# A mixture-of-experts weight stream with 16 raw and 4 high buffers, blocks in TensorE's order of use

## What is computed

```python
def swiglu(t, w_up, w_down):
    gate, up = split_cols(t @ w_up, (w_down.shape[0], w_down.shape[0]))
    return (jax.nn.silu(gate) * up) @ w_down

y = swiglu(u_pad[tok], w_exp_up[e], w_exp_down[e])      # up: 1024 x 512, down: 256 x 1024
acc = acc.at[tok].add(y.astype(jnp.float32) * w_of_slot[slots][:, None])
```

## Time and profile before

| | us |
|---|---|
| runs | 1229.41, 1229.84, 1231.94 |
| median | 1229.84 |
| the profiled execution | 1231.59 |
| its span | 1229.3 |
| TensorE busy (matmuls) | 1137.4 |
| VectorE busy | 900.8 |
| ScalarE busy | 723.1 |
| GpSimd busy | 222.1 |

### The profile page before, as it was taken

How to read it: one execution, slowest core, us unless ns; L and a number is a source line. 1 busy time by engine, 2 the same in 40 slices (tenths; PEclk the granted TensorE clock), 3 DMA queues, 4 the chain that set the end, 5 groups by cost and what they waited for, 6 DMA issues and landing times.

```text
span 1229.3 us, 16284 instructions
## 1 busy us (share of the span) xinstructions
PE 1137.4 (93%) x5707; PEld 860.9 (70%) x5707; DVE 900.8 (73%) x1133; ACT 723.1 (59%) x926; POOL 222.1 (18%) x145
## 2 busy tenths in 40 slices
PE   4999998989999899998999999999999999999893
PEld 3699997766777688774666666666666667666662
DVE  4585468544433576578899999998989899999881
ACT  7543343333333422413788888888878788888781
POOL 1000000000000000001232333333433233333421
PEclk9999999999999999999999999999999999999997
DMA  6413232221212234267899999999999999999982
GB/s 214 134 53 103 86 95 69 69 69 34 68 35 68 81 120 137 86 257 272 298 355 362 366 364 369 367 362 369 375 370 368 370 366 378 373 377 362 370 291 33
DMA packets 74495, 285.58 MB, mean 232 GB/s; under 512 B 10868, under 2 KB 33416, under 8 KB 49620
## 3 DMA queue, kind: packets, MB, share of 16 engines
q1 hardware_dynamic: 59716, 251.16, 54.2%
q0 software_dynamic: 14736, 33.87, 11.6%
HBM read 272.39 MB, written 29.38 MB: 245 GB/s over the span
## 4 chain that ended last, share of the span: by engine, by line
PE 58%; DMA 14%; DVE 12%; ACT 7%; issue 7%; SPq 0%; DVEq 0%; POOL 0%; ACTq 0%; POOLq 0%
PE bank L1452 47%; DMA arena<-in_w_exp_up_dram 12%; DVE low L1356 4%; ACT high L554 4%; DVE gatheredT L1363 2%; PE bank L1620 2%; DMA out_dram<-arena 2%; ACT arena L554 2%; PE bank L1647 2%; PE bank L1833 1%; PE bank L1531 1%; PE bank L1778 1%; PE bank L1632 1%; DVE arena L1370 1%; DMA arena<-in_x_dram 1%
## 5 line engine op out<-in xcount | busy, mean ns | idle before, releaser
L1356 DVE TENSOR_TENSOR low<-arena,high 128x2048 fp32r<-128x2048 f32 x192 | 435.3, 2287 | 51.7 <-ACT high L554 51.5
L554 ACT ACTIVATE high<-arena 128x2048 fp32r<-128x2048 f32 x192 | 363.9, 1918 | 23.0 <-DMA arena<-in_w_exp_up_dram 22.2
L1452 PE MATMUL bank<-high,gatheredT 128*96 128x512 f32 x1024 | 327.0, 401 | 19.2 <-DVE gatheredT L1363 17.9
L516 POOL DMA_INDIRECT arena<-u_rows,arena x64 | 103.3, 1614 | 742.1 <-DVE arena L1351 563.5
L1452 PEld LDWEIGHTS bank<-high,gatheredT 128*96 128x96 f32 x1024 | 161.5, 163 | 93.2 <-issue 23.9
L1452 PE MATMUL bank<-low,gatheredT 128*96 128x512 f32 x512 | 203.2, 397 | 0.0
L1452 PE MATMUL bank<-high,hidT 128*96 128x512 f32 x512 | 163.6, 401 | 1.5 <-ACT arena L554 1.5
L524 POOL DMA_INDIRECT out_dram<-arena x64 | 112.7, 1761 | 250.1 <-DMA out_dram<-arena 148.5
L1452 PE MATMUL bank<-hT_high,front_split 128*128 128x512 f32 x448 | 146.4, 409 | 0.8 <-DVE hT_low L892 0.8
L554 ACT ACTIVATE arena<-bank 96x512 f32<-96x512 f32 (+4 forms) x217 | 107.7, 533 | 62.9 <-PE bank L1452 28.3
L1452 PEld LDWEIGHTS bank<-low,gatheredT 128*96 128x96 f32 x512 | 83.4, 163 | 36.5
(11 more groups left out here) (253 smaller groups left out, 1402.5 us busy)
## 6 DMA issues: line engine op xcount, KB each, us to landing
arena<-in_w_exp_up_dram SPq DMA_DIRECT2D x128, 1024.0 KB, 22.7
arena<-in_w_exp_down_dram SPq DMA_DIRECT2D x64, 1024.0 KB, 18.8
arena<-in_w_in_dram SPq DMA_DIRECT2D x14, 1024.0 KB, 5.4
arena<-in_w_in_dram SPq DMA_DIRECT2D x10, 768.0 KB, 4.4
arena<-in_w_branches_dram SPq DMA_DIRECT2D x4, 1024.0 KB, 5.0
arena<-in_w_out_dram SPq DMA_DIRECT2D x4, 1024.0 KB, 5.0
arena<-in_x_dram SPq DMA_DIRECT2D x4, 512.0 KB, 5.5
arena<-in_w_mem_kv_dram SPq DMA_DIRECT2D x2, 1024.0 KB, 5.0
```

The lines of the kernel that those rows point to most:

```text
L516: pool.indirect_dma_start(gathered[0:ROWS, e % 2, :], None, u_dram, bass.IndirectOffsetOnAxis(ap=index[0:ROWS, e:e + 1], axis=0), bounds_c ...
L554: return nc.scalar.activation(o, i, ACT.Copy, **kw)
L1356: v.tensor_tensor(low_part[q % SLOTS], raw[q % SLOTS], high_part[q % HIGHS].bitcast(F32), ALU.subtract).then_inc(low_done, 1)
L1452: ins = mm(bank, left[a], right[b], start=first and q == 0, stop=last and q == 2)
```

## The change

- `SLOTS` 12 to 16 and `HIGHS` 6 to 4: two high buffers and the places of routing data (`gates_at` + 4096 and + 6144, `ib_at`, `ib_at` + 2048) become raw buffers. `place`, `w_high`, `w_low` and the token numbers move to other corners, since loads now land where they were.
- Blocks are numbered by position in TensorE's order of use: up 0, up 1, down 0, up 2, down 1, ... (`up_at`, `down_at`). Loads, conversions and products all take buffers by this position.
- A load at position k waits for `block_used` to reach k - 15, that is for the block that had its buffer. In the first round positions 10 and 11 wait for `set_done`, 12 and 13 for `folded`, 14 and 15 each for two of the output stores, which now have two semaphores.
- Stores of output rows: two after the load at position 10, then a wait until the first gather has landed (`gather_in[0]`), then loads 11 to 13, then the other two stores.
- A conversion waits for `block_used` of the block four positions before it.
- `TURN` 4 to 16: 16 experts written out at the start, a loop of two turns (SyncE: three), 16 at the end. The old `TURN` that sized the routing tables becomes `DEAL` = 4.

Cut to its core:

```diff
-TURN = 4
+DEAL = 4
+TURN = 16
 BLOCKS = 3
-SLOTS, HIGHS = 12, 6
-LEAD = 5
+SLOTS, HIGHS = 16, 4
+ROUNDS = BLOCKS * TURN // SLOTS
...
+def up_at(n, j, first=False):
+    return j if first and n == 0 else BLOCKS * n - 1 + j
+
+def down_at(n, last=False):
+    return BLOCKS * n + (2 if last and n == TURN - 1 else 4)
...
-            def load_expert_block(e, n, j, u0):
-                s = (BLOCKS * n + j) % SLOTS
-                if not isinstance(e, int):
-                    sp.wait_ge(block_used, u0 + (BLOCKS + 2 - SLOTS if j == 2 else j - SLOTS + (n == 0)))
...
+            def load(src, k, u):
+                s = k % SLOTS
+                if not isinstance(u, int) or k >= SLOTS:
+                    sp.wait_ge(block_used, u + (k - SLOTS + 1))
+                elif s < 4:
+                    sp.wait_ge(x1_done, 2 * NT)
+                elif s < 6:
+                    sp.wait_ge(front_low, S0 + s - 3)
+                elif s < 10:
+                    sp.wait_ge(s_up, NT)
+                elif s < 12:
+                    sp.wait_ge(set_done, 1)
+                elif s < 14:
+                    sp.wait_ge(folded, 1)
                 else:
-                    sp.wait_ge(out_stored, 16 * NT)
+                    sp.wait_ge(out_stored[s - 14], 16 * NT // 2)
+                sp.dma_start(raw[s].rearrange("p k n -> p (k n)"), src).then_inc(raw_in[s], 16)
+
+            def store_rows(k, u):
+                if isinstance(u, int) and k in (10, 13):
+                    for t in (0, 1) if k == 10 else (2, 3):
+                        sp.wait_ge(out_ready, t + 1)
+                        sp.dma_start(out[0, t * P:(t + 1) * P, :], x_tok[:, t, :]).then_inc(out_stored[t // 2], 16)
+                    if k == 10:
+                        sp.wait_ge(gather_in[0], 16)
+
+            def load_turn(e, n, u, first=False):
+                for j in range(2):
+                    load(up_src[:, e, j, :], up_at(n, j, first), u)
+                    store_rows(up_at(n, j, first), u)
+                if not first or n:
+                    load(dn_src[:, e - 1, :], down_at(n - 1), u)
+                    store_rows(down_at(n - 1), u)
...
+            def high(k, u, round0):
+                if isinstance(u, int) and u + k < HIGHS:
+                    act.wait_ge(s_up, NT)
+                else:
+                    act.wait_ge(block_used, u + (k - HIGHS + 1))
+                act.wait_ge(raw_in[k % SLOTS], round0 * 16 + 16 * (k // SLOTS + 1))
+                copy(high_part[k % HIGHS], raw[k % SLOTS]).then_inc(high_done, 1)
...
             def expert(n, m, u, round0, start=False, last=False):
...
-                for j in range(min(blocks, 2)):
-                    high(q + j, u + (LEAD + j), round0)
+                if ups:
+                    high(up_at(n + 2, 0), u, round0)
+                    high(up_at(n + 2, 1), u, round0)
...
-                if blocks > 2:
-                    high(q + 2, u + (LEAD + 2), round0)
+                if downs:
+                    high(down_at(n + 1, last), u, round0)
```

More of the change, by code:

```diff
@@ L180, in build @@
         s_hid = at(qa_at, NT, FH)
-        ro = [at(ib_at + n * 256, NT, E) for n in range(16)]
-        (score, choice, masked, masked2, picked, weight, place) = ro[0:7]
+        (score, choice, masked, masked2, picked, weight) = [at(ib_at + n * 256, NT, E) for n in range(6)]
+        place = at(square_at + P, NT, E)
         router_bias = at(ib_at + 11 * 256, E)
@@ new lines, in load_turn, with load_pass @@
+            def load_turn(e, n, u, first=False):
[5 more added lines that the diff above has]
+                    store_rows(down_at(n - 1), u)
+            def load_pass(u0):
+                for n in range(TURN):
+                    load_turn(n, n, u0, True)
+                with sp.Fori(1, E // TURN) as g:
+                    for n in range(TURN):
+                        load_turn(g * TURN + n, n, u0 + g * (BLOCKS * TURN))
+                load(dn_src[:, E - 1, :], BLOCKS * TURN - 1, u0 + BLOCKS * (E - TURN))
@@ L474, in _ @@
                     with sp.If(fullest > r * ROWS):
[L475 to L479 removed]
+                        sp.wait_ge(index_ready, r + 1)
+                        load_pass(r * (BLOCKS * E))
         @block.gpsimd
@@ L535, in expert_pass @@
                     if isinstance(r, int) and e == 0:
-                        pool.wait_ge(out_stored, 16 * NT)
+                        for h in range(2):
+                            pool.wait_ge(out_stored[h], 16 * NT // 2)
                     scatter(e, r)
@@ L823, in expert @@
             def expert(n, m, u, round0, start=False, last=False):
-                q, blocks = BLOCKS * n + LEAD, ahead(n, last)
+                ups, downs = not last or n + 2 < TURN, not last or n + 1 < TURN
                 act.wait_ge(hidT_done, m + 1)
```

170 lines of the change are left out of this document (72 added, 98 removed).

## The result

The changed kernel takes 1243.61 us (median of 4 runs, 1242.35 to 1247.3), the kernel before beside it 1229.62 (4 runs, 1228.5 to 1231.94). The ratio is 1.0117, 95% interval 1.0092 to 1.0141: slower by 14 us, where 9 us faster was forecast. The profiled execution has a span of 1241.7 us.

A forecast was written before the change was run, and what follows sets the result against it. DMA and TensorE were both full, with DMA taken to set the end. A 3.25 MB head start at 367 GB/s gives 8.9 us, other costs zero or hidden: 1229.84 - 8.9 = 1220.9 us, range 1216.9 to 1229.0.

The forecast's parts named there:

- The bytes: Loads before 603.8 us: earlier issue and fuller DMA give a head start of 3.25 MB.
- ScalarE's waits for loads: Sign of being right: conversions' waits for loads fall from 22 us to under 8, all late.
- From bytes to time: End of the DMA-limited experts: 3.25 MB at 367 GB/s moves it 8.9 us earlier.
- The bound for the high ring: Conversions with 4 high buffers: closed loop of 9.5 us against 9.605, costing 0 to 0.05 us per expert.
- the third rival: Head start lost again through longer gather or scatter waits or SyncE idling: 1229 to 1231, no change; chance 0.11.
- Turns of 16: Loops of 16 experts: same instructions, fewer jumps; 1 us taken, hidden by later DMA waits.
- the second rival: Long loop body stalls an engine on an instruction fetch at expert 32: about 1225; chance 0.14, shared with tighter high buffers.
- Order of use: Conversions permuted into TensorE's order: more slack, no gain by itself, cost zero.
- The hold: SyncE holds loads 11 to 15 and last stores until the first gather lands, in 4.0 to 4.8 us: cost zero.
- the cushion of late loads: Some 3 us of remaining DMA waits in the last experts, hiding up to 3 us of PE, ScalarE or VectorE costs.

The follow-up runs named there:

- a_rot: Changed kernel with loops rotated by two experts, so experts 2 to 49 are real loop code on TensorE, VectorE and ScalarE: median 1239.5 us (1223.73 to 1245.11).
- b_t16_two: Kernel before with turns of 16 and a second DRAM sum for odd experts' scatters, final sum of the two left out: 1230.0 us.
- a_two: Changed kernel with odd experts' scatters into a second DRAM sum, so two can be in flight, final sum left out: 1225.5 us.
- b_turn16: Kernel before with turns of 16 experts instead of 4, nothing else changed: 1247.3 us, ratio 1.0134.
- a_t4: Changed kernel with turns of 4 instead of 16 and hence 12 raw buffers: 1226.5 us, ratio 0.9979.
- a_t4_nohold: Changed kernel with turns of 4 and 12 raw buffers, loads and stores no longer waiting for the first gather: 1232.4 us.
- a_slow2: Changed kernel with two redundant TensorE transposes more in every expert: 1251.2 us (1242.14 to 1251.85).
- a_dynpe: Changed kernel with TensorE's experts 2 to 15 in a loop of one pass, which was built without register steps: 1246.6 us.
- a_lowsplit: Changed kernel with each of VectorE's long subtractions cut into two halves: 1241.3 us (1235.5 to 1248.53).
- a_slow1: Changed kernel with one redundant TensorE transpose more in every expert: median 1236.2 us (1225.67 to 1247.53).
- b_t16_rot: Kernel before with turns of 16 and its loops rotated by two experts: 1246.8 us (1243.03 to 1255.71).
- b_peelpe: Kernel before with TensorE's first 16 experts as straight code instead of the first 4: median 1234.1 us (1226.38 to 1241.51).
- a_t4_lowsplit: Changed kernel with turns of 4, 12 raw buffers and VectorE's subtractions cut in two: 1227.4 us.

## Why the prediction was wrong

**What held.** The bytes: 564 to 603.8 us ran at 340 GB/s instead of 242, which is 3.9 MB in 39.8 us, against 3.25 forecast. Some of it is chance. In this execution VectorE took over the routing products at 563.64, 2.9 us earlier than before, though the work up to there is the same; over the profiles of all kernels this instant lies between 562.4 and 568.9.

```profile
563.64 1.49 DVE L1358 TENSOR_TENSOR own_part<-bank,arena 128x432 fp32r<-128x432 f32 x3 [0.36 <-PE bank L1831]
```

Counted from there, over 37.2 us each, it is 334 GB/s against 238, or 3.6 MB. DMA share 1.02 and 381 GB/s up to 603.8; ScalarE's waits for loads are gone; conversions wait 1.7 us at the longest for the ring of 4, 7.6 us in all; the loop jumps stay at 76 to 211 ns.

**From bytes to time** the forecast was too high even without the chain. The short execution of a_rot, with all parts of the change, has a span of 1221.9 against 1229.3, 7.4 us less; counted from the routing products on (564.43 and 566.57) it is 5.2. With the chain cut, the change without its turns is worth 1230.0 - 1225.5 = 4.5 us (b_t16_two and a_two). Forecast were 8.9, so about half of this term came. Where the rest went no run shows; in a_two loads are late again, 16.0 us in 14 waits. The bound for the high ring was added up a little low as well: with halves of 1.86 and 2.28 us the loop makes 9.55, not 9.5.

**The step that failed** is the third rival's, in two places. "Scatters already land in 8.9 us, longest 10.5, near the period of 9.6, and they run one after the other": the period of a scatter is not its landing but its landing and the 0.8 us until the next one starts, and with that it was 9.67 in the first stretch of before (600 to 690 us, below): 0.7 us of slack per expert became next to none. I had compared a duration with a period.

```profile
L524 POOL DMA_INDIRECT out_dram<-arena x10: 1442/1442/1792, 600.3 to 687.3; - x10
...
DMA to landing us min/median/max: 8.1/8.7/9.6
```

(687.3 - 600.3) / 9 = 9.67. The chain could do slightly better than that: over the next 13 experts, up to 820.8 us, it kept to (820.8 - 696.6) / 13 = 9.55:

```profile
L524 POOL DMA_INDIRECT out_dram<-arena x14: 1442/1442/1751, 696.6 to 820.8; - x14
```

In the second place I wrote of scatters of 9.7 us that "the pace would be theirs: 1229 to 1231, no change", and against it "the DMA share is 1.02 in both versions, so their competition is the same". The landing does not hang on the DMA share alone. At the same share of 1.02 it was 8.7 us where scatters lag by 6 us (a_rot) and 9.4 where they lag by 10 (the changed kernel), with issues of 1.47 and 1.90. Without the issues that is 7.2 and 7.5, so the larger part of the difference is how long VectorE holds up GpSimd, a cost that the DMA share doesn't show. So the chain, once it sets the pace, is slower than the pace that it takes over, and the result is a loss. What was missing was a rival that says so: from expert 16 on 47 x (10.19 - 9.6) = 28 us behind a pace of 9.6, where late loads cost the kernel before 12.3.

**Turns of 16** were the term of the sum that was mis-sized: 1 us forecast, 17 measured in the kernel before (b_turn16), and some 2 without the chain (b_t16_two). I looked for the cost in jumps and code fetches, the second rival. There was none: what the turns did first was a gain, 0.09 us per expert, and it goes with the fewer register steps (a_rot, in loop code, is back at 9.62). TensorE can't use it, as the scatters don't follow.

**Order of use and the high ring**: order, ring and hold together, with 12 buffers, are worth 3.3 us (a_t4), in the direction forecast and not to be told further apart. **The hold** was put at no cost, since the gather "lands in 4.0 to 4.8 us when DMA is light". That held: in a_t4 it lands in 4.1, and without the hold the kernel is 5.9 us slower (a_t4_nohold), of which the later first tokens are 2.9.

**The range** ended at 1229 because every cost that I let stand was bounded by the cushion of late loads. But the cushion of the scatters, the third resource near its limit, was not worked out at all.

**When the lag jumps.** In the profiles of kernels with one chain the lag of the scatters stays below 2 us (before, for 49 experts), rests at 6 to 8, or at 9 to 11, and at 9 to 11 the result copies wait. The expert at which it first passes 9 goes with the time of that execution:

| profiled execution | lag first over 9 at expert | us |
|---|---|---|
| a_slow2 | 11 | 1250.7 |
| a_dynpe | 13 | 1250.0 |
| the changed kernel | 14 | 1243.5 |
| a_lowsplit | 26 | 1235.5 |
| a_slow1 | 50 | 1225.7 |
| a_rot | never | 1223.7 |
| a_t4 | never | 1225.4 |

So the wide spreads within a series need no third cause: it is enough that the jump comes sooner or later. One profile a kernel can't prove that.

**What stays open.** Shown: the changed kernel's time is set by the chain of scatters (a_two, b_t16_two), a scatter comes every 9.7 or every 10.2 us in the profiles, and turns of 16 bring on the second in most executions. Only argued: why. Pace alone doesn't decide (a_slow2, b_t16_rot), nor does straight code alone (b_peelpe, a_rot). Whether the issues that VectorE lengthens decide, a_lowsplit can't tell, since its halves often held them up like one subtraction. That the second began at expert 9, inside a subtraction, is one observation in one profile. The best complete version is a_t4, the change with turns of 4 (a_t4_lowsplit is the same within the spread): 1226.5 us, 0.2% below the kernel before.

## What to carry over

For a chain of transfers that wait for each other, compare its whole period (issue, landing, hand-off) with the pace of the loop, before giving any other engine a gain: here 9.55 to 9.67 against 9.6, and 0.09 us less elsewhere turned into 0.6 more. When two resources are full and a third is within 1% of the pace, its slack is a term of the sum, and so is what happens to its own durations once it is late. A change to loop shape (straight code, long bodies) changes the pace too; where something marginal hangs on it, time it alone first.

## What the runs showed of the hardware that I had not expected

- A scatter of half the bytes, with the other half in flight beside it, lands no sooner under saturated loads: 9.1 us (median of 120) for 96 rows of 2 KB, 9.1 for 96 rows of 4 KB (median of 58, the changed kernel in 600 to 1190 us); with few loads left a whole one landed in 4.9.
- GpSimd's issue of a scatter took 1.44 us alone. Begun while VectorE ran its subtraction of 2.29 us (two SBUF inputs), it ended 1.32 us after that subtraction, in all 36 cases of the changed kernel with more than 0.15 us of it left, so it took up to 3.46 us; one that began 0.3 us before a subtraction took 3.9. Two subtractions of half the length back to back held up twelve issues of a_lowsplit like one.
- In loop code TensorE stopped for 0.4 us before a weight load 15 times in some 17 experts (5.9 us, none of it in a wait that the profile shows), in straight code twice; 0.09 us per expert of it shows in the pace. That these are the register steps is inferred. A loop jump over 16 experts took 0.21 us at most.
- One program (a_rot) ran for 1223.7 and for 1245.1 us within one series on one chip. The profiles of its short execution and of the changed kernel differ by the lag of the scatters, not by the clock (0.983 and 0.985 in the mean) or the DMA share (1.02).
